# The order of mask and score products in the attention units of a hybrid decoder layer

## The reference

```python
# native sparse attention, 8 query heads, 2 key heads; for the selected and for the window branch
s = einsum(q, k) * SCALE
p = softmax(where(kpos <= t, s, NEG_INF))          # causal
o = einsum(p, v)
# dilated attention, 8 heads; three dilations, mixed by their log-sum-exp
mask = (dist >= 0) & (dist <= max_dist)
s = where(mask, einsum(q, k) * SCALE, NEG_INF)
out = sum over the dilations of softmax(lse) * (softmax(s) @ v)
```

## Time and profile before

| | |
|---|---|
| time, median of 3 runs | 1479.71 us |
| the three runs | 1479.66, 1479.71, 1485.19 us |
| span of the profiled execution | 1485.9 us |
| its mean granted TensorE clock | 0.968 of 2.4 GHz |
| PE busy | 1335.0 us, 90% of the span |
| PE, weight loads | 776.0 us, 52% |
| DVE busy | 645.0 us, 43% |
| ACT busy | 315.4 us, 21% |
| POOL busy | 188.5 us, 13% |
| moved between HBM and the core | 506.02 MB, mean 341 GB/s |

### The profile page before, as it was taken

The page is one execution under the profiler, slowest core; times in us unless marked ns, Lnnn a source line. Parts: engine busy times, 40 slices in busy tenths (PEclk is TensorE's granted clock), DMA queues, the critical chain, the costliest instruction groups (busy, mean ns, idle before and its releaser), DMA issues.

```text
span 1485.9 us, 44835 instructions
## 1 busy us (share of the span) xinstructions
PE 1335.0 (90%) x18595; PEld 776.0 (52%) x18602; DVE 645.0 (43%) x1704; ACT 315.4 (21%) x840; POOL 188.5 (13%) x265
## 2 busy tenths in 40 slices
PE   5999999999978999988989978899999999989973
PEld 2464555655545555554555544455555555545531
DVE  2558446785562433333333323243344334333344
ACT  2120014664320121111212111112111211111211
POOL 0300003443000010000101000001000100010131
PEclk9999999999988999999999989999999999999996
DMA  9758308302469999999999999999899899999995
GB/s 354 269 204 290 123 0 331 151 1 113 185 257 422 407 402 423 424 425 426 426 425 407 409 426 427 424 426 405 352 427 426 331 400 426 425 425 425 424 384 192
DMA packets 77344, 506.02 MB, mean 341 GB/s; under 512 B 9596, under 2 KB 16228, under 8 KB 52728
## 3 DMA queue, kind: packets, MB, share of 16 engines
q1 hardware_dynamic: 66624, 474.96, 77.9%
q0 software_dynamic: 6560, 20.00, 3.6%
q10 hardware_dynamic: 4120, 10.51, 1.8%
HBM read 473.90 MB, written 31.53 MB: 340 GB/s over the span
## 4 chain that ended last, share of the span: by engine, by line
PE 63%; DMA 28%; DVE 4%; issue 2%; another core or an unknown queue 1%; SPq 1%; ACT 1%; POOL 0%; ACTq 0%; DVEq 0%; POOLq 0%
PE ps L1871 25%; DMA arena<-in_w_down 24%; PE ps L1891 14%; PE ps L1528 7%; PE ps L1784 4%; DMA arena<-in_w_in 2%; PE ps L1636 2%; PE ps L1675 2%; PE ps L1715 1%; PE ps L1495 1%; PE ps L1879 1%; DVE arena L910 1%; DMA arena<-in_w_ada 1%; PE ps L1643 1%
## 5 line engine op out<-in xcount | busy, mean ns | idle before, releaser
L1871 PE MATMUL ps<-arena 128*32 128x256 f32 x10240 | 584.9, 382 | 39.6 <-issue 28.5
L1871 PEld LDWEIGHTS ps<-arena 128*32 128x32 f32 x10240 | 342.0, 111 | 259.6 <-issue 53.6
L1891 PE MATMUL ps<-arena 128*32 128x256 f32 x5120 | 308.4, 392 | 42.4 <-DMA arena<-in_w_down 42.4
L1350 DVE TENSOR_SCALAR arena<-ps 128x128 f32<-128x128 f32 x160 | 46.8, 292 | 578.3 <-PE ps L1879 573.3
L1891 PEld LDWEIGHTS ps<-arena 128*32 128x32 f32 x5120 | 157.9, 112 | 169.0 <-issue 53.6
L825 ACT ACTIVATE arena<-ps 32x256 f32<-32x256 f32 x320 | 120.1, 375 | 330.0 <-PE ps L1891 309.4
L819 ACT ACTIVATE arena<-arena 128x128 f32<-128x128 f32 x160 | 49.7, 311 | 519.2 <-DVE arena L1350 519.2
L603 POOL DMA_INDIRECT arena<-xn_rows,arena x81 | 78.9, 974 | 482.3 <-DVE arena L1320 396.3
L1528 PE MATMUL ps<-arena 128*128 128x512 f32 (+1 forms) x320 | 129.7, 561 | 3.1 <-DMA arena<-in_w_in 3.1
L1528 PEld LDWEIGHTS ps<-arena 128*128 128x128 f32 x320 | 60.3, 192 | 64.0 <-issue 56.1
L589 POOL TENSOR_SCALAR arena<-arena 128x128 f32<-128x128 f32 (+3 forms) x48 | 51.7, 1082 | 223.3 <-DVE arena L1122 201.6
(11 more groups left out here) (328 smaller groups left out, 977.8 us busy)
## 6 DMA issues: line engine op xcount, KB each, us to landing
arena<-in_w_up SPq DMA_DIRECT2D x128, 2048.0 KB, 16.9
arena<-in_w_down SPq DMA_DIRECT2D x64, 2048.0 KB, 29.2
arena<-in_w_ada SPq DMA_DIRECT2D x12, 2048.0 KB, 11.5
slot_rows<-arena SPq DMA_DIRECT2D x4, 3328.0 KB, 25.6
arena<-in_w_in SPq DMA_DIRECT2D x5, 2048.0 KB, 10.8
slot_rows<-arena ACTq DMA_DIRECT2D x80, 128.0 KB, 6.1
arena<-in_w_o SPq DMA_DIRECT2D x2, 2048.0 KB, 11.0
arena<-in_x SPq DMA_DIRECT2D x4, 512.0 KB, 5.2
```

The source lines that it names most:

```text
L1871: ins = pe.matmul(out_of(y, g), xgT[:, 2 * n + k, :], tiles[par][n][:, k, at:at + 256], start=(n == 0 and k == 0), stop=False)
L1891: ins = pe.matmul(out_of(5, g), actT[:, y, k, :], tiles[par][4 + y][:, k, 256 * g:256 * (g + 1)], start=False, stop=(y == 1 and k == 3))
```

## The change: what it does

In `qk(u)` the two loops change places. The mask products come first: the first of them in each bank clears it (`start`), and the scores are added to them; the last score product raises `qk_done`. The number and the shapes of the instructions, the banks, the waits and everything on other engines stay as they are.

```diff
                 b = (u + 1) % 2 * 2
                 for i, at in rows:
                     for h in range(2):
-                        dims = slice(HD * h, HD * h + HD)
-                        q = (qdil[dims, pr - 4] if ty == N_DIL else qrot[dims, pr])[:, i * P:(i + 1) * P]
-                        k = (kdil[dims, pr - 4] if ty == N_DIL else (kslc, kwin)[ty][dims, pr // 2])[:, 0:P * (i + 1)]
-                        pe.matmul(ps[:, b + h, span(i, at)], q, k, start=(at == 0), stop=False)
-                for i, at in rows:
-                    for h in range(2):
                         if ty == N_DIL:
                             dst, mask = span(i, at), mb_b[:, (3 - i) * P:512]
                         else:
                             dst, mask = span(0, at + i), trib
-                        ins = pe.matmul(ps[:, b + h, dst], identb, mask, start=False, stop=(i == rows[-1][0]))
+                        pe.matmul(ps[:, b + h, dst], identb, mask, start=(at == 0), stop=False, skip_group_check=True)
+                for i, at in rows:
+                    for h in range(2):
+                        dims = slice(HD * h, HD * h + HD)
+                        q = (qdil[dims, pr - 4] if ty == N_DIL else qrot[dims, pr])[:, i * P:(i + 1) * P]
+                        k = (kdil[dims, pr - 4] if ty == N_DIL else (kslc, kwin)[ty][dims, pr // 2])[:, 0:P * (i + 1)]
+                        ins = pe.matmul(ps[:, b + h, span(i, at)], q, k, start=False, stop=(i == rows[-1][0]),
+                                        skip_group_check=True)
                 ins.then_inc(qk_done, 1)
```

## The result

The changed kernel takes 1474.0 us (median of 9 runs, 1470.96 to 1477.15). The kernel before, run beside it, takes 1479.78 us (9 runs, 1476.67 to 1485.19). The medians differ by 5.8 us. The ratio is 0.9960, with a 95% interval of 0.9946 to 0.9973, which is 4.0 to 8.0 us. The forecast was 2.6 us less, 1477.1, in a range from 1474.7 to 1483.0. It is faster by less than half a percent, as forecast, but by more than twice the amount.

What follows compares the result with a forecast made beforehand. Attention was taken as bound by PE from 245.6 to 318.5 us, then by DVE. 26 passages at 0.10 us save 2.6 us, so 1479.7 - 2.6 = 1477.1 us, range 1474.7 to 1483.0.

Steps and rivals of the forecast that it cites:

- The bound and the hand-overs: In attention: PE bounds until 318.5 us, then DVE; PE's hand-over to another form costs 0.09 to 0.10 us.
- Part 1: Masks ahead of scores: transposes to masks costs nothing, the gap between scores and masks goes, saving 0.10 us a step.
- Part 2: Scores to values: changing both rows and columns costs 0.09 to 0.10 us, with bounds of zero and 0.20.
- Part 3: Mask's 98 ns weight load behind transposes: hidden under the last one; if not, it costs 0.10 us, saving nil.
- Parts 4 to 6: In qk: no cost from waiting for exp_done or clearing a bank by masks; qk_done moved to scores starts DVE's maximum sooner.
- How often it counts: Passages through the masks in attention's chain: 1 + 2 + 20 + 3 = 26, at 0.10 us each, 2.6 us.
- The rival on the clock: Attention's 1.2 GHz stretch or run level changes: 1475.5 if it disappears, 1480.3 with two more, 1482.6 at higher level; chance 0.12.
- The range: Whole kernel's median: 1474.7 to 1483.0 us, held at 8 in 10.
- What the profile after would show: Step 8, transposes to values, shrinks from 2.30 to 2.20 us; turn(4) to unit 26's scores shrinks by 2.0 us.

Runs made afterwards that it cites:

- e3_half_first: Changed kernel with only the first head's masks ahead of the scores, the second head's behind them; 1483.41 us against 1484.39 of the kernel before, ratio 0.9995.
- after: First profile of the changed kernel, all masks first, against the kernel before; median 1474.0 us against 1479.78, ratio 0.9960.
- e2_after_again: Changed kernel run again with no edit; 1479.44 us against 1484.39 of the kernel before, ratio 0.9967, 4.9 us less, between 2.4 and 7.4.
- e4_pad: Changed kernel with 13 products of 512 columns added behind the last unit's values; ratio 0.9968 of the kernel before.
- e7_pad65: Changed kernel with 65 products of 512 columns added between attention and the output projection; ratio 1.0058 of the kernel before, 8.6 us above it.
- e8_before_third: The kernel before, unchanged, profiled a third time; 1480.2 us (8 runs) against 1479.86.

## Why the prediction was wrong

**The bound and the hand-overs: right.** The chain, PE's packed stretch, DVE's stretch from unit 27 on and the price of a hand-over, read from starts at 0.09 to 0.10 us, all hold. `e3_half_first` shows that the price belongs to the hand-over, not to the masks.

**Part 1, masks first: right.** 0.106 us a passage against 0.10.

**Part 2, scores to values: right in the value taken.** 92 ns; neither bound (zero or 0.20) came.

**Part 3, the mask's weight load: right.** 109 ns from transpose to mask, so it is hidden. The Trainium skill's rule in "TensorE: Matmul & The Clock Gate" ("The mechanism"), that weight loads overlap running products only when their row groups differ, doesn't hold for these forms: both take all 128 rows. The Trainium skill's statement in "TensorEngine Tiling (Array Packing)" ("Key Properties"), that changing the tiling mode drains TensorE, agrees, and each change costs 92 to 96 ns here.

**Parts 4 to 6: right.** No new wait at `exp_done` (the masks come 109 ns behind the transposes), the maximum starts sooner, clearing by the mask costs nothing (the second mask follows at 56 ns, where it was 66).

**How often it counts: nearly right.** 26 passages at 0.10 were 2.6 us, measured 2.85. Of this 2.75 lies between `turn(0)` and `turn(35)`, where the rounds of the dilated units gave 0.44 in place of 0.3. The share of unit 1 lies ahead of `turn(0)`: from the start of line 1528's last product to `turn(0)` it is 4.68 us in the seven profiles with unit 1's masks all first and 4.78 in the seven others.

**The clock: the step that failed.** The rival on the clock had the size right, 1.6 us for the stretch and 1475.5 for its absence. Its cause and its chance were wrong. I put it down to PE's idle 0.78 us before `turn(4)`, so I took it for an accident of one execution, left its 1.6 us out of the sum and gave the disturbed reading 0.12. That idle time, 0.78 or 0.79 us, stands before `turn(4)` in all 14 profiles, and the clock fell behind the first group in two of them. One such stretch was there in each of three executions of the kernel before, each time behind a group of line 1701, and in none of the four with all masks first (`after`, `e2_after_again`, `e4_pad`, `e7_pad65`); by chance that would come once in 35. So its removal very likely comes with this edit, though how is not shown. With it the forecast would have read 2.85 + 1.6 = 4.45 us, 1475.3 from the median shown. Between `turn(4)` and the fall of the clock stood the narrow products, in step 4, which the rows ahead of the prediction don't show. Timeline of PE, the kernel before:

```profile
247.49 2.19 PE L1701 MATMUL ps<-arena 32*64 32x512 f32 x4
```

The first result speaks for the term, since 2.85 us lies outside its interval of 4.0 to 8.0; the second (2.4 to 7.4) allows both.

**The range: too narrow below.** The other 1.3 us, from 1475.3 to 1474.0, I can't put down to anything that the edit does; they lie within the interval, and the kernel before differed by 2.5 us from itself in one set. The kernel before has medians of 1479.8, 1484.4 and 1479.9 us in three sets, and single executions of one kernel in one set spread over 5 to 12 us. The profiles show where: up to 4 us ahead of attention, 6 us in the experts, and 9 us behind them, where ACT's last pieces come 0.3 to 13.5 us late. A range on nine runs would have needed some 2 us for this on either side. I had taken it on the upper side only, from the three runs shown.

**What the profile after would show** came as written for the order, the 0.92 and 0.52 us and the 2.19 us of step 8. The sentence that the stretch shrinks by 2.0 us held without the clock: the steps from `turn(4)` to `turn(24)` gave 2.1, and 1.63 more came in step 5.

## What to carry to other kernels

Count the changes of form (rows by columns) in a loop of products: each cost 0.09 us here, and groups with the same form put side by side cost nothing, whatever their types, and with a wait that is already met. Read such prices from starts between two marks in the trace, since a stretch repeated to 0.03 us where the whole kernel scattered over 10. And when the clock falls in a stretch where TensorE is busy, look at what stood right ahead of it, in several executions of both kernels, before calling it an accident.

## What the runs showed of the hardware

- A change of form costs the same 92 to 96 ns from 128*128 to 64*128 or 128*64, from either back to 128*128, from 64*128 to 128*64, and from 128*128 or 64*128 to 32*64.
- Weight loads of 98 ns (bfloat16, 128 rows) hide under float32 transposes that use the same rows: 109 ns from start to start.
- The granted clock fell to 1.2 GHz with TensorE busy 3.28 of the 3.40 us before it by the profile (`e8_before_third`), behind four products on 32 rows and 64 columns that took 2.25 us from start to start for 1.71 us of stream. It cost 1.6 us each time.
- A count raised by TensorE's last products of the experts released ACT 0.3 to 0.4 us behind the last of them in five of the 14 profiles and 4.8 to 13.5 us behind in nine; in 13 profiles the trace has the count itself 0.13 us ahead of ACT (in `e2_after_again` it has none ahead); the stretch from the last product of the experts to the end was 43 to 46 us up to 7.8 us of delay, and 48 to 52 us above. Its cause wasn't looked for.
